# Filler matmuls on TensorE at two phase changes of a decoder-layer kernel

## The reference

```python
hp = _rmsnorm(xp, norm_mix_g[l])
q, lat, kpe, gb, u = _mixer_inputs(hp, w_in[l], q_lora_g[l], kv_lora_g[l], w_uq[l],
                                   q_norm_g[l], cos_p, sin_p)
k, v = _expand_kv(lat, kpe, w_ukv[l], k_norm_g[l])
attn = _prompt_attention(q, k, v)
up = jnp.concatenate([jnp.zeros((B, CONV_W - 1, CONV_CH), u.dtype), u], axis=1)
conv = _short_conv(up, gb, conv_w[l], conv_b[l])
xp = _merge_and_ffn(xp, attn, conv, attn_out_g[l], conv_out_g[l], w_o[l],
                    norm_ffn_g[l], w_up[l], w_down[l])
```

## Time and profile before

| | us |
|---|---|
| median of 3 runs | 1947.84 (1943.69 to 1948.97) |
| the profiled execution, device time | 1952.36 |
| its span, first to last instruction | 1950.6 |
| PE busy in the span | 1893.9 (97%) |
| DVE, ACT, POOL busy | 918.1, 726.2, 524.6 |

### The profile page before, as it was taken

How to read it: one execution, slowest core, us unless ns; L and a number is a source line. 1 busy time by engine, 2 the same in 40 slices (tenths; PEclk the granted TensorE clock), 3 DMA queues, 4 the chain that set the end, 5 groups by cost and what they waited for, 6 DMA issues and landing times. The chain is left out here.

```text
span 1950.6 us, 35503 instructions
## 1 busy us (share of the span) xinstructions
PE 1893.9 (97%) x12628; PEld 1794.0 (92%) x12628; DVE 918.1 (47%) x1725; ACT 726.2 (37%) x1530; POOL 524.6 (27%) x472
## 2 busy tenths in 40 slices
PE   6999998999989999999999999999999999999998
PEld 5999996777679999999999899999999999999998
DVE  5116134777647777777777433222222222323132
ACT  5111223666656666666667322111111111111111
POOL 3232323333112322333321153222222212122221
PEclk7999998999889999999999999999999999999999
DMA  6122100000212222222222321111111202020203
GB/s 230 44 68 66 23 10 20 1 1 0 71 49 63 74 71 71 74 74 73 73 73 63 111 57 42 43 45 54 32 54 32 65 26 81 5 81 11 76 17 106
DMA packets 183991, 108.77 MB, mean 56 GB/s; under 512 B 52516, under 2 KB 179586, under 8 KB 183764
## 3 DMA queue, kind: packets, MB, share of 16 engines
q1 hardware_dynamic: 183718, 107.14, 19.3%
q10 hardware_dynamic: 174, 0.30, 0.1%
HBM read 97.40 MB, written 10.00 MB: 55 GB/s over the span
## 5 line engine op out<-in xcount | busy, mean ns | idle before, releaser
L2215 PE MATMUL banks<-comb_hi,pageT_hi 128*128 128x272 f32 x1024 | 233.7, 309 | 0.0
L2076 DVE TENSOR_REDUCE k_sums<-k_sq 128x8 f32<-128x512 f32 x256 | 174.2, 680 | 90.8 <-ACT k_sq L1868 90.5
L2215 PE MATMUL banks<-comb_hi,pageT_lo 128*128 128x272 f32 x1024 | 212.3, 289 | 0.0
L2215 PE MATMUL banks<-comb_lo,pageT_hi 128*128 128x272 f32 x1024 | 212.2, 289 | 0.0
L2633 DVE TENSOR_TENSOR x_kept<-x_kept,banks 128x1056 f32<-128x1056 f32 x64 | 80.3, 1254 | 272.1 <-PE banks L248 272.1
L1868 ACT ACTIVATE k_sq<-banks 128x512 f32<-128x512 f32 x256 | 152.4, 595 | 138.3 <-PE banks L2215 136.0
L237 POOL TENSOR_TENSOR w_down_lo<-w_down_raw,w_down_hi 128x512 fp32r<-128x512 f32 x64 | 94.4, 1476 | 342.4 <-ACT w_down_hi L233 342.4
L237 POOL TENSOR_TENSOR w_out_up_lo<-w_out_up_raw,w_out_up_hi 128x1024 fp32r<-128x1024 f32 x40 | 100.7, 2524 | 312.3 <-ACT w_out_up_hi L233 312.3
L2491 ACT ACTIVATE a_hi<-relu 128x1056 fp32r<-128x1056 f32 x32 | 34.9, 1089 | 386.5 <-DVE relu L2621 386.5
L248 PE MATMUL banks<-hf_hi,w_out_up_hi 128*128 128x352 f32 x768 | 166.3, 324 | 0.0
L248 PE MATMUL banks<-a_lo,w_down_hi 128*128 128x352 f32 x768 | 165.9, 324 | 0.0
(11 more groups left out here) (399 smaller groups left out, 3807.3 us busy)
## 6 DMA issues: line engine op xcount, KB each, us to landing
page_latents<-in_cache_kv_latent SPq DMA_DIRECT2D x256, 128.0 KB, 2.0
w_out_up_raw<-in_w_up SPq DMA_DIRECT2D x32, 512.0 KB, 4.7
w_down_raw<-in_w_down SPq DMA_DIRECT2D x64, 256.0 KB, 2.8
w_in_raw<-in_w_in SPq DMA_DIRECT2D x17, 512.0 KB, 3.9
x_spill<-xT SPq DMA_DIRECT2D x1, 4296.0 KB, 14.1
x_kept<-x_spill SPq DMA_DIRECT2D x8, 528.0 KB, 8.8
page_ropes<-in_cache_k_rope SPq DMA_DIRECT2D x256, 16.0 KB, 1.8
w_out_up_raw<-in_w_o SPq DMA_DIRECT2D x8, 512.0 KB, 5.0
```

The costliest lines, as they stand in the source:

```text
L2076: nc.vector.tensor_reduce(ksum[par][:, j, :], sq[j % 2][:, :].rearrange("p (h c) -> p h c", h=H), AX_X, ALU.add)\
L2215: mm = pe.matmul(banks[:, 2 * (j % 2) + half, 0:WC], x[j % AHEAD][:, k, :], w[par][:, k, half, :], start=k == 0 and a == 0, stop=k == KL - ...
```

## The change

A helper issues a number of matmuls of ones by ones, 128x128 float32 with 128 columns, whose result nobody reads. It is called three times: 10 times behind the last transposes of the input phase (into bank 0), 16 times ahead of the first transposes of prompt attention (into bank 7), and 10 times behind the last products of prompt attention (into bank 0). The two waits ahead of the calls make sure that bank 0 has been read by ScalarE.

```diff
@@ inputs, block.tensor, at its end
             for c in range(KL):
                 mm = pe.transpose(banks[:, 6, c * NS:(c + 1) * NS], g.new_page[0:NS, c * P:(c + 1) * P], ident[0:NS, 0:NS])
             mm.then_inc(latT_done, 1)
+            pe.wait_ge(q_copied, NT)
+            keep_busy(g, pe, 0, 10)
+
+
+def keep_busy(g, pe, bank, times):
+
+    for _ in range(times):
+        pe.matmul(g.banks[:, bank, 0:P], g.ones[:, :], g.ones[:, :], start=True, stop=True)
@@ prompt_attention, block.tensor
             def loop(n, par, *_):
                 if isinstance(n, int) and n == -1:
+                    keep_busy(g, pe, UNIT_BANK, 16)
                     for u in range(NU):
                         transpose_unit(0, u, 2 + u)
                     pe.wait_ge(s["ready"], 3)
...
             loops(pe, loop)
+            pe.wait_ge(s["copied"], H * NB)
+            keep_busy(g, pe, 0, 10)
```

## The result

Over 14 runs of each kernel the median is 1951.82 us with the change and 1948.16 without, 3.7 us apart. One of the 14 runs of the changed kernel took 9123.96 us at a mean granted clock of 0.19; nothing here explains it, and the ratio leaves it out. The ratio of the two kernels, which is an estimate from all other runs and not the quotient of the medians, is 1.0024 (95% interval 1.0017 to 1.0031), 4.7 us slower. A second comparison, with 11 runs of the changed kernel, gave 1.0014 (1.0005 to 1.0023), 2.8 us, with medians 3.4 us apart. The forecast was 1951.0, and slower by 3.2 us.

The account below looks back on a forecast made before the run. PE, busy for 97% of the span, and its granted clock were taken to bound the kernel. Terms 1.4 + 3.9 - 1.1 + 0.5 - 1.5 = +3.2 us on the 1947.84 median gave 1951.0; range 1944.5 to 1956.5.

Parts of the forecast that it names:

- First call: Ten fillers ahead of the first barrier, at half speed, end after VectorE's arrival: +1.4 us, between 0 and +1.8.
- Second call: Sixteen fillers ahead of the first transposes, 11 at half speed and 5 at full, less 2.4 us of cover: +3.9 us.
- my signs of being wrong: No clock fall around 331 us, second-call fillers under 0.3 us, barrier opening while PE multiplies, or no half speed 522 to 543.
- What the clock gives back there: Transposes and scores behind the sixteen fillers run at full speed: -1.1 us, between 0 and -2.3.
- the lower end: Behind the sixteen fillers the clock falls again while PE waits over 2 us for VectorE: gain 0.
- Third call: Ten fillers ahead of the second barrier at full speed cost +0.5 us; shorter half speed behind it gives -1.5, at most -3.0.
- The early and held clock: Rival: clock rises during the first ten fillers and holds past both barriers; sum -2.4 us, 1945.4; chance 0.17.
- The clearly slower case: Rival: clock stays at half through all sixteen fillers before the first transposes, nothing comes back; +8.1 us, 1955.9; chance 0.16.
- The shift against whatever times the clock: Rival: the half-speed stretch from 522.5 to 543.0 in prompt attention goes although unchanged; sum -4.8 us, 1943.0; chance 0.08.

Follow-up runs that it names:

- the first experiments: Four kernels: only the 10, only the 16 or only the last 10 fillers kept, or six in the last head instead; against before 1.0002, 1.0002, 1.0005, 0.9986.
- the chain of fillers: Against the kernel before: 6, 4 and 13 fillers up to the first barrier, 10 behind it, 10 before first scores, 7 before the second barrier; ratio 1.0001.

## Why the prediction was right, step by step

**First call.** Forecast +1.4, shown +1.18 in all four profiles that have it (A 3.01 or 3.02 against 1.84). The fillers ended where the sum had them, 1.42 us behind VectorE; a filler at half speed took 0.43 to 0.44 us where I took 0.45. The missing 0.2 us is in the barrier, which opened 1.37 us after TensorE's last end, and 1.61 us after VectorE's when VectorE was last. The question that I left open, whether the barrier waits for the matmuls in flight, is answered yes.

**Second call.** Forecast +3.9, shown +2.6, +2.9 and +2.95 (B). This term was the most mis-sized. Two numbers were too large: 11 fillers at half speed, where 7 or 8 were, since the clock came back 3 to 3.6 us into the call; and 0.27 us at full speed, read from two matmuls with other instructions behind them, where a long row runs at 0.22 to 0.23. Fillers shorter than 0.3 us in the second call stood among my signs of being wrong, although my own sum had five of them at 0.27; eight or nine ran at 0.22, and that sign was badly chosen.

**What the clock gives back there.** Forecast -1.1 between ends of 0 and -2.3. C shows -0.87 and the scores nothing: the clock fell again in the wait for VectorE, as the lower end had it, but the transposes gained more than the 0.5 us that I gave them. Over the profiles, C + D is 180.42 to 180.59 in the four kernels with the second call of 16 or 32, and 180.26 to 182.11 (mean 181.3) in the five profiles without fillers at the first barrier: -0.8. The two ranges overlap, but C alone, 4.65 or 4.66 against 5.26 to 5.52, gives the same 0.8. One argument of the prediction goes too far here: that the trace disagrees with the Trainium skill, "TensorE: Matmul & The Clock Gate", section "Part 4: PE-mode transpose". The clock did rise at 17.3 over transposes alone, but eight records of transposes take 1.74 us at half speed, 0.22 each like those of fillers, and no run here shows whether they go in the mode of which that section speaks.

**Third call.** Forecast +0.5 and -1.5. The cost is +0.45 in each profile with ten. The gain is -1.7 between the first two profiles, but G is 8.03 to 9.50, mean 9.1, in the seven profiles with third-call fillers and 9.08 to 10.80, mean 9.8, in the six without: about -0.7, and with ranges that overlap this far it is not shown to differ from nothing. I had taken one execution's 6.8 us at half speed as the kernel's; its other two profiles have 3.4.

**The sum** with these sizes is 1.18 + 2.75 - 0.8 + 0.45 - 0.7 = +2.9 us, 0.15%, which the second comparison's 1.0014 meets; the first one's interval begins at 3.3 us. What the difference of 0.4 us or more consists of, luck of 14 runs or a step that I do not follow, stays open. That the forecast of +3.2 came so near is in part luck, because its two larger errors went opposite ways: the second call was priced 1.1 us too high and the gain at the second barrier 0.8 too high.

**The rivals.** The early and held clock did not come in the two profiles of the changed kernel, where it came back within the second call. It came in part elsewhere: with 32 fillers in the second call, and the first call as in the change, it was back at 337.2 and stayed until 350.9. So some executions of the changed kernel may run that way; how many is not known. The clearly slower case did not come either: the clock came back before the sixteenth filler each time. The shift against whatever times the clock was real, but it is no effect of the change: the stretch from 522 to 543 was there in the changed kernel's first profile, shorter in its second, and gone in the third profile of before.

## What to carry to other kernels

A filler matmul costs nothing only while something else is waited for: count the gap, divide by the price at the clock that is granted there (0.43 us at half speed, 0.22 at full, for 128x128 float32), and stop short of it; beyond it each one is on the path, and ahead of a barrier it holds up all five engines. Put fillers where a fall would be followed by much work at half speed: six of them ahead of 20 us of products were worth 2.7 us (1.0 to 4.5), 36 around two short stretches lost 3 to 5. And profile the unchanged kernel more than once before reading a clock stretch as its property.

## What the hardware showed that was not expected

The same kernel, unchanged, had 20.5, 6.8 and 0 us at half speed in its last head, worth 25.48, 19.33 and 16.06 us of time; together with H (9.04 to 13.67) that is more than the whole effect of this change. The time ahead of A varies as well: VectorE's L876 starts at 334.89 to 337.28 us in the three. Over the 35 runs of before beside the first experiments, which spread from 1943.5 to 1952.5 us, the time goes with the mean granted clock: the six runs at 0.981 or less took 1951.7 to 1952.5 us, the seven at 0.986 took 1943.5 to 1946.3. A piece of 2.6 us in which TensorE stood idle for 1.5 us and did eight small products was followed by a fall of the clock in one execution (first profile of before) and not in another (third). Full speed was lost inside a barrier in the chain of fillers (at 335.9, with TensorE idle from 333.8 to 336.4), and came back inside one with 32 fillers in the second call (at 337.2, with TensorE idle from 336.8 to 338.2).
